# One-core transformer kernel: two batches of transposes and one batch of small matmuls change places with plain matmuls

## The reference

```python
def reference(...):
    x = first_block(x, mem, positions, ...)
    return second_block(x, c_2, ctx_2, c_ctx_2, ...)

# first_block, at the two places that the change touches
h = h + merged @ w_out
h = h + memory_cross_attention(rmsnorm(h, norm_cross_g), rmsnorm(mem, norm_mem_g), ...)
h = h + peer_ffn(rmsnorm(h, norm_ffn_g), w_peer_q, sub_keys, peer_u, peer_v)
...
return rmsnorm(h, norm_final_g)

# second_block
ada = einsum('bd,lde->lbe', silu(c), w_ada) + b_ada      # "modulation", 6 x 1024 values
hc = modulate(rmsnorm_2(ctx, norm_mix), csh1, csc1)      # the context, times w_in[:, :1536]
...
h = modulate(rmsnorm_2(x, norm_mix), sh1, sc1)
o = token_mixers(h @ w_in, ...)
```

## Time and profile before

| | us |
|---|---|
| three runs | 1989.83, 1990.62, 1995.02; median 1990.62 |
| the profiled execution | 1989.83, of which the span of the trace is 1988.0 |
| PE busy | 1872.8 (94%) |
| PE weight loads | 1590.2 (80%) |
| DVE, ACT, POOL busy | 1237.4, 920.5, 642.7 |
| DMA | 343.41 MB, 173 GB/s on average |

### The profile page before, as it was taken

The page is one execution under the profiler, slowest core; times in us unless marked ns, Lnnn a source line. Parts: engine busy times, 40 slices in busy tenths (PEclk is TensorE's granted clock), DMA queues, the critical chain, the costliest instruction groups (busy, mean ns, idle before and its releaser), DMA issues.

```text
span 1988.0 us, 33389 instructions
## 1 busy us (share of the span) xinstructions
PE 1872.8 (94%) x11448; PEld 1590.2 (80%) x11448; DVE 1237.4 (62%) x2242; ACT 920.5 (46%) x1279; POOL 642.7 (32%) x305
## 2 busy tenths in 40 slices
PE   6999987999989999999999999999999999889996
PEld 5998866895765899999999988888884765549996
DVE  2477776632212399457777588888883656637776
ACT  4556623443433544467777533333333652214443
POOL 5887523785332688820000000000000013103333
PEclk9999987999999999999999999999999999999998
DMA  5554401456534467665655787777777533225553
GB/s 185 191 180 161 136 22 49 158 185 226 167 124 137 142 178 216 201 184 175 179 172 172 216 260 236 238 237 237 236 234 271 169 98 102 77 106 181 188 181 104
DMA packets 121685, 343.41 MB, mean 173 GB/s; under 512 B 13777, under 2 KB 46673, under 8 KB 121361
## 3 DMA queue, kind: packets, MB, share of 16 engines
q1 hardware_dynamic: 120096, 335.32, 52.5%
q0 software_dynamic: 1520, 7.21, 1.0%
HBM read 324.65 MB, written 17.83 MB: 172 GB/s over the span
## 4 chain that ended last, share of the span: by engine, by line
PE 61%; POOL 3%; DVE 2%; issue 2%; ACT 1%; DMA 1%; POOLq 0%; DVEq 0%; ACTq 0%
PE banks L846 61%; POOL weight_rest L742 3%; DMA weight_ring<-in_stream 1%; ACT weight_high L1385 1%; PE banks L857 0%; ACT arena L1385 0%; DVE arena L2386 0%; DVE weight_rest L2183 0%; DVE act_feature_major L1844 0%; ACT scratch L1385 0%; DVE residual L2359 0%; DVE arena L2357 0%; DVE act_feature_major L1847 0%; ACT L1385 0%; POOLq L383 0%
## 5 line engine op out<-in xcount | busy, mean ns | idle before, releaser
L1385 ACT ACTIVATE weight_high<-weight_ring 128x1024 fp32r<-128x1024 f32 x436 | 460.9, 1057 | 452.9 <-PE banks L846 410.9
L742 POOL TENSOR_TENSOR weight_rest<-weight_ring,weight_high 128x1024 fp32r<-128x1024 f32 x204 | 520.9, 2561 | 234.0 <-ACT weight_high L1385 157.5
L2183 DVE TENSOR_TENSOR weight_rest<-weight_ring,weight_high 128x1024 fp32r<-128x1024 f32 x232 | 284.1, 1225 | 181.9 <-ACT weight_high L1385 174.0
L846 PE MATMUL banks<-a_high,weight_high 128*128 128x256 f32 x1216 | 304.7, 288 | 0.2 <-ACT weight_high L1385 0.2
L846 PE MATMUL banks<-a_rest,weight_high 128*128 128x256 f32 x1216 | 298.6, 283 | 0.0
L1385 ACT ACTIVATE arena<-banks 128x512 f32<-128x512 f32 (+4 forms) x262 | 172.9, 681 | 158.2 <-PE banks L846 155.7
L846 PEld LDWEIGHTS banks<-a_rest,weight_high 128*128 128x128 f32 x1216 | 233.5, 192 | 0.5 <-issue 0.5
L846 PEld LDWEIGHTS banks<-a_high,weight_high 128*128 128x128 f32 x1216 | 233.1, 192 | 0.9 <-issue 0.5
L846 PE MATMUL banks<-weight_high,gated_high 128*128 128x512 f32 x512 | 201.4, 393 | 0.0
L846 PE MATMUL banks<-weight_high,gated_rest 128*128 128x512 f32 x512 | 200.2, 391 | 0.0
L846 PE MATMUL banks<-a_high,weight_rest 128*128 128x256 f32 x1216 | 172.7, 285 | 13.1 <-POOL weight_rest L742 13.1
(11 more groups left out here) (292 smaller groups left out, 3244.1 us busy)
## 6 DMA issues: line engine op xcount, KB each, us to landing
weight_ring<-in_stream SPq DMA_DIRECT2D x504, 512.0 KB, 3.5
arena<-in_stream SPq DMA_DIRECT2D x66, 512.0 KB, 3.3
unit_spill<-small SPq DMA_DIRECT2D x128, 128.0 KB, 3.7
scratch<-unit_spill SPq DMA_DIRECT2D x128, 128.0 KB, 3.3
residual<-in_x SPq DMA_DIRECT2D x2, 512.0 KB, 4.0
arena<-in_mem POOLq DMA_DIRECT2D x2, 512.0 KB, 4.8
arena<-in_ctx POOLq DMA_DIRECT2D x2, 512.0 KB, 5.1
arena<-in_keys POOLq DMA_DIRECT2D x1, 1024.0 KB, 5.1
```

The source lines that it names most:

```text
L742: nc.gpsimd.tensor_tensor(w_lo[:, e % 2, :], raw(e)[0], w_hi[:, e % 2, :], ALU.subtract).then_inc(S["rest_ready"], 1)
L846: return nc.tensor.matmul(out, lhsT, rhs, start=start, stop=stop, skip_group_check=True)
L1385: return nc.scalar.activation(out, in_, f, **kw)
L2183: tt(w_lo[:, e % 2, :], raw(e)[0], w_hi[:, e % 2, :], ALU.subtract).then_inc(S[ready], 1)
```

## The change

In three places the order of PE's work is altered, and the lists of banks and ACT's evacuations follow.

- Place A: all four `modulation_rows(0, j)` come first, then the transposes a2T. Before, two came first, then the transposes, then the other two.
- Place B: `token_block("ctx", 2, ...)` comes ahead of the transposes a3T, not behind them. On ACT, `evacuate_ctx(2)` is ahead of the high quarters.
- Place C: all four `modulation_rows(1, j)` come ahead of the transposes x2T, and PE's two waits for the parts of x2 now stand ahead of `modulation_turned(1, j)`. Before, they stood behind it.

No instruction is added or removed. DVE's, POOL's and SP's programs are unchanged, and the stream of weights as well.

```diff
--- before.py
+++ after.py
@@ -234,13 +234,11 @@
     for b in range(2):
         for t in range(TT):
             B.job("wo", b, t)
-    for j in range(2):
+    for j in range(4):
         B.job("ad0", "rows", j)
     for t in range(TT):
         for h in range(2):
             B.job("a2T", t, h)
-    for j in range(2, 4):
-        B.job("ad0", "rows", j)
     for j in range(4):
         B.job("ad0", "turned", j)
     for n in range(8):
@@ -268,10 +266,10 @@
         for h in range(2):
             B.job("y", t, h, bank=2 * t + h)
     for t in range(TT):
+        B.job("cp", 2, t, bank=6 + t)
+    for t in range(TT):
         for h in range(2):
             B.job("a3T", t, h, bank=4 + 2 * t + h)
-    for t in range(TT):
-        B.job("cp", 2, t, bank=6 + t)
     B.loop("pq", 2, 8, banks=(4, 5, 6, 7, 4, 5, 6, 7))
     for t in range(TT):
         for q in range(4):
@@ -287,13 +285,11 @@
     B.loop("u2", U_GATED // 4, 4, banks=(4, 5, 4, 5))
     B.loop("w", T // 16, 4, banks=(6, 7, 6, 7))
     B.loop("u3", U_LATE // 4, 4, banks=(4, 5, 6, 7))
-    for j in range(2):
+    for j in range(4):
         B.job("ad1", "rows", j, bank=4 + j)
     for t in range(TT):
         for h in range(2):
             B.job("x2T", t, h, bank=2 * t + h)
-    for j in range(2, 4):
-        B.job("ad1", "rows", j, bank=4 + j)
     for j in range(4):
         B.job("ad1", "turned", j)
     for b in P_ORDER:
@@ -1095,11 +1091,9 @@
                 filled(ins, (f"ad{q}", "turned", j))
 
             pe.wait_ge(S["silu_c"], 1)
-            for j in range(2):
+            for j in range(4):
                 modulation_rows(0, j)
             norm_transposes("a2T", XN, 3)
-            for j in range(2, 4):
-                modulation_rows(0, j)
             for j in range(4):
                 modulation_turned(0, j)
             both_ready("a2", 4)
@@ -1150,8 +1144,9 @@
                     b = claim(("y", t, h))
                     ins = mm(b, ident, hres[:, t, h * 512:(h + 1) * 512], start=True, stop=False)
             ins.then_inc(S["y_seeded"], 1)
+            token_block("ctx", 2, "cp", CXT)
+
             norm_transposes("a3T", XN, 5)
-            token_block("ctx", 2, "cp", CXT)
             both_ready("a3", 4)
             with pe.Fori(0, 2) as i:
                 for j in range(8):
@@ -1253,15 +1248,13 @@
             for a in range(P - 4, P):
                 values(a, last=(a == P - 1))
 
-            for j in range(2):
+            for j in range(4):
                 modulation_rows(1, j)
             norm_transposes("x2T", XN, 7)
-            for j in range(2, 4):
-                modulation_rows(1, j)
+            pe.wait_ge(S["x2_hi_ready"], 4)
+            pe.wait_ge(S["x2_lo_ready"], 4)
             for j in range(4):
                 modulation_turned(1, j)
-            pe.wait_ge(S["x2_hi_ready"], 4)
-            pe.wait_ge(S["x2_lo_ready"], 4)
             for n, b in enumerate(P_ORDER):
                 split_block(I0 + 4 * n, "p", b, x2_hi, x2_lo)
             for t in range(TT):
@@ -1618,9 +1609,9 @@
                 split_high(E0["cross_out"] + m)
             norm(5, lambda t: hres[:, t, :], lambda t: XN[:, t, :], lambda t: [freed(act, ("cw", b, t)) for b in range(2)])
             evacuate_ctx(1)
+            evacuate_ctx(2)
             act.wait_ge(S["y_seeded"], 1)
             high_quarters("a3T", a3_hi, lambda n: freed(act, ("a3T", n // 2, n % 2)), "a3_hi_ready")
-            evacuate_ctx(2)
             split_high(E0["peer_q"] + 1)
             for n in range(16):
                 split_high(E0["peer_q"] + n + 2)
```

## The result

The changed kernel took 2004.83 us, the median of 8 runs (2000.47 to 2012.68), against 1993.74 us for the kernel before in 8 runs on the same chip (1989.83 to 1996.37). The ratio is 1.0053, with a 95% interval of 1.0040 to 1.0066: slower by 8 to 13 us. The profiled execution of the changed kernel took 2004.6 us around a span of 2002.8 us, 14.8 us more than the span of before.

What follows compares the result with a forecast made beforehand. The prediction took PE at its matmul line, 61% of the chain that ended last, as the bound. A 0.0, B 3.8 and C 8.6 gave +12.4 us on 1989.83; it took 2002.5 us, range 1996.3 to 2008.

Steps and rivals of the forecast that it cites:

- The frame: Whole kernel: microseconds PE waits at a passage between two layers are mostly microseconds of the kernel; sum +12.4 us.
- A, 0.0: Place A: the turning behind the transposes covers the rest of the path to the operands; cost 0.0, bounds 0 and +1.9.
- ring that starves: Place A: sixteen weight tiles in a row without the transposes' pause could slip; upper bound +1.9 us, taken as 0.
- B, +2.0 without clock, +1.8 with it: Place B: a3 ready 2.7 us later, less 0.7 for POOL's wait; half clock after PE's idle time adds 1.8.
- C, waits +4.9: Place C: PE idles some 6.5 us until x2 is ready, no tile wait; the projection starts 4.9 us later.
- C, turning +3.2: Place C: the turning runs at the half clock after the idle time, 6.8 us instead of 3.65; +3.2, bounds 0 and +3.6.
- C, +0.5 in the projection: Place C: the half-clock stretch in the projection costs 1.4 to 2.4 us instead of 1.4; taken as +0.5.
- 1 (no further clock): Places B and C: waits as worked out, but the clock doesn't react further; +6.9 us, 1996.7; chance 0.17.
- 2 (half level used up by the wait): Place C: the half level is gone when the projection starts, the turning limited by issue; +5.5 us, 1995.3; chance 0.10.
- 3 (ring starves): Places A and C: four weight slots can't keep up without the pause; +1.9 us each on the forecast, 2006.3; chance 0.12.
- 5 (removed waits decide): Places B and C: removed waits of 1.53, 1.31 and 0.7 us make it 3.5 us faster, 1986.3; chance 0.05.
- 4 (transposes don't count as activity): Place A: transposes and turning make 5.6 quiet us, the turning slows by up to 3.2 us; 2005.7; chance 0.06.

Runs made afterwards that it cites:

- e1: The kernel before with only place A's part of the change; 1993.82 us, ratio 0.9999 to the kernel before.
- e4: The changed kernel with the two waits for x2 back behind the turning at place C; 1997.91 us, ratio 1.0016 to the kernel before.
- e6: The changed kernel with extra matmuls on constants, results unused, in PE's waits at C and B; 1998.65 us, ratio 1.0028 to the kernel before.
- e2: The kernel before with only place B's part of the change; 1997.75 us, ratio 1.0017 to the kernel before.
- e3: The kernel before with only place C's part of the change, waits for x2 ahead of the turning included; 1999.51 us, ratio 1.0028.
- e7: The kernel before with POOL's 256 KB and 1 MB transfers issued after the last modulation row at C; 1988.22 us, ratio 0.9980.
- e8: e7 plus, at place B, the transposes a3T ahead of the four seeding matmuls; 1987.38 us, ratio 0.9978 to the kernel before.
- e9: The kernel before with the turning at A and C in two halves, between rows 2 and 3 and behind them; 1988.18 us, ratio 0.9983.
- e10: The edits of e8 and e9 together; 1987.38 us, ratio 0.9972 to the kernel before.

## Why the prediction was right, step by step

**The frame.** That each microsecond PE stands still at a passage is one of the kernel's held: nothing between or behind the places took it back. Of the profiled pair's 14.8 us, 0.9 arose ahead of A, 0.1 at A, 4.4 at B, 7.9 at C and 1.4 behind C, where the changed kernel has one more stretch at 0.50 from 1598.7; the first and the last were not in the sum, and no run explains them. The forecast of +12.4 on one profile, and of 2002.5 on the median, stands against 8 to 13 and 2004.8. Measured from the 1990.62 I started at, the ratio gives 2001.2, from the 1993.74 of the comparison 2004.3; the forecast lies between. It is closer to the measured median than its parts are, and that is luck: the median that I started from, of three runs, was 3.1 us below that of eight, and the change of 11.9 was above the 10.6 that the ratio gives. Either alone stays inside the range.

**A, 0.0.** Right: 0.14 us in the profiled pair, 0.9999 (0.9982 to 1.0015) in e1. The projection did not start at 510.9 because the whole had shifted by 0.9. The bound of +1.9 for a ring that starves was not needed: 64 records took 27.74 us, 0.43 each, and at C 60 took 25.91; the longest time lost there was 0.3 us (28.04 for the 64 in e4, a wait of 0.25 in e6).

**B, +2.0 without clock, +1.8 with it.** Right in mechanism: transposes last, 4.06 us of wait ended by DVE, no bank wait, no wait for POOL, half level behind it. The sum of 3.8 met 4.4 (from the start of the context block ahead of B to the end of the projection, 83.98 to 88.36) and 3.4 from e2. Three terms were off by little. The projection started 3.1 us later, not 2.7 (33.79 and 36.86 us behind the start of that block): the first matmul came 637.38 - 636.94 = 0.44 us behind DVE's end, where I had 0.1, and it did so in e6 at the full clock too. The removed wait for POOL was worth more than 0.7: in e6, at the full clock, the projection takes 49.06 us where it took 50.19 before, 1.1 less. And the half level cost 2.4 us, not 1.8; it held for 6.8 us, like the bound from the earlier trace rows and not like the usual 3.4.

**C, waits +4.9.** Right: transposes to turning 8.60 us (8.50 + 0.1), idle 6.63 (6.5), no tile wait.

**C, turning +3.2.** Right: 6.88 us between starts against the 6.8 worked out, from 3.65. The ratio of 1.87 taken from transposes carries over to the turning. My reason, "128-row weight loads", was put wrongly: the operand of the turning is 2 rows by 128 columns (`2*128`), and what the two have in common is a weight load 128 columns wide for every record. That these loads set the pace was not tested. e6 shows that it is the clock: with PE at work in the wait, 3.63.

**C, +0.5 in the projection.** Not there: the part of the half stretch that lies in it is 3.0 us long, where it was 3.4.

**What I had mis-sized: C in the kernel before.** I took C's removed wait as 1.53 us, the one value that the trace had, and 35.95 us as what C takes. Four executions in that order gave waits of 1.53 to 3.25 us, the longer ones with a fallen clock behind them, and 37.9 us on average. The change takes that away too, so C's cost is on average nearer 6 us than 7.9 (8.1 by my terms); e3's interval, 2.6 to 8.8 us, holds all of them. e7, which removes only that wait, won 4.0 us (2.2 to 6.0) where the trace of before had a wait of 1.53, and that points the same way. The prediction's sentence "it came behind POOL's transfer" was right, as e7 shows; what was missing is that this wait has no fixed length and needs a range of its own.

**The rivals.** 1 (no further clock) and 2 (half level used up by the wait) fall with the 13.7 us at 0.50 and with e6. 3 (ring starves) falls with the records' pace. 5 (removed waits decide) falls with the sign; its parts are real, though: without the bank wait and the tile wait, but with the rows kept behind the transposes, e7 and e8 are faster by 0.2%. 4 (transposes don't count as activity) is not borne out at the size it claimed. In the changed kernel the turning at A took 3.73 us at full pace, directly behind 1.97 us of transposes. The turning at A was drawn out in two of the four executions with transposes directly ahead of it (4.5 us in e1, 5.0 in e6) and in two of the six with rows between (4.2 in e3, 4.7 in e7). Nor does the half level come earlier: with transposes directly ahead it began 2.2 to 5.0 us behind the start of the turning (five cases, e4 at C with the four at A), with rows ahead 2.2 to 5.2 (twelve cases at A and C). If the 1.9 us of transposes were quiet time, one would expect it earlier there. The Trainium skill, page "TensorE: Matmul & The Clock Gate", Part 4 (PE-mode transpose), says that transposes don't count as PE being busy in the same way; these traces don't agree with it, though so few executions can't exclude a small part of it.

**What stays open.** Why the clock falls inside the turning in one execution and behind it in the next was not found, nor why e9 keeps A's half stretch and e10 does not. C's average cost is known only between 2.6 and 8.8 us, and which of POOL's two transfers held up the tile is not known.

## What to carry to other kernels

Before moving filler work ahead of a chain of transposes, copies and splits on other engines, measure that chain from its first matmul to its last operand, and ask what the matmul engine has left to do beside it; the kernel loses the uncovered rest, and the clock can charge half as much again (here 10.7 us of new waits and 5.4 of clock, less what the removed waits had cost). A short block of small matmuls is the right cover only if its own wait does not stand in front of it. And a wait caused by a transfer beside another transfer should be read from several executions before its removal enters a sum.

## What the runs showed of the hardware

- **The spread of a kernel's runs goes with the granted clock.** 35 runs of the kernel before beside e1 to e4 reach from 1989.49 us at a mean clock of 0.978 to 2002.81 at 0.971; the five above 1999 us have 0.971 to 0.973, the other thirty 0.976 to 0.979. From the ends that is 0.007 x 2 x 2000 = 28 us more at the half level; at the 1 - 18/30 = 0.4 that such time loses by the earlier trace rows it makes 11 of the 13 us, by estimate. What brings the clock down in a run was not found.
- **The clock falls at a block through which PE is busy.** The turning, 32 records of 2x2 with a weight load each, has PE busy without a gap, and a half stretch came at it in 20 of 20 cases; cut in two (e9, e10), in 1 of 4. What in the block brings it was not tested. Where it began behind the turning (9 cases, twice) it held 3.4 us; where it began inside (9 cases) it held 6.8 us and drew the turning out; where it began in a wait ahead (C of the changed kernel and of e3) 13.7 us. A case of the second kind in the old order is e3 at A, where the turning runs from 508.85 to 513.08, in the columns of the earlier trace rows:
```profile
511.90:518.70 6.80, 6.80 (x33) 6.78 (x33) 0.59 (x5) 2.30 (x4) 2.38 (x1) 0.50 0.19 63
```
That is part of what makes two executions of one order differ here: 33.2 us against 33.8 at A.
- **Rows records keep the clock.** 64 in a row with only two rows of result ran at 0.43 us each for 27.74 us and the clock stayed at 1.00.
- **A wait for a tile beside POOL's transfers varied twofold,** 1.53 to 3.25 us between four executions, with 256 KB and 1 MB on POOL's queue beside SP's 512 KB tiles; with these two held back until the rows were done, it was gone (e7, e8).
